# Two down projections of each feed-forward as seven half-size block products per pair of panels

## The reference

```python
# first block
h = h + (jax.nn.silu(f @ w_gate[i]) * (f @ w_up[i])) @ w_down[i]
# second block
u = causal_dwconv(h2 @ w_ff_up[l], conv_ff_w[l], conv_ff_b[l])   # 3 taps over positions
gate, val = jnp.split(u, 2, axis=-1)
x = x + (jax.nn.silu(gate) * val) @ w_ff_down[l]
```

## Time and profile before

| | us |
|---|---|
| median of 3 runs (1553.41 to 1555.92) | 1555.33 |
| span of the profiled execution | 1553.9 |
| TensorE busy in it | 1539.9 (99%) |
| GpSimd busy | 905.7 (58%) |
| Vector busy | 747.5 (48%) |
| Scalar busy | 395.1 (25%) |

### The profile page before, as it was taken

The page is one execution under the profiler, slowest core; times in us unless marked ns, Lnnn a source line. Parts: engine busy times, 40 slices in busy tenths (PEclk is TensorE's granted clock), DMA queues, the critical chain, the costliest instruction groups (busy, mean ns, idle before and its releaser), DMA issues.

```text
span 1553.9 us, 22779 instructions
## 1 busy us (share of the span) xinstructions
PE 1539.9 (99%) x7847; PEld 1291.7 (83%) x7847; DVE 747.5 (48%) x1157; ACT 395.1 (25%) x757; POOL 905.7 (58%) x536
## 2 busy tenths in 40 slices
PE   8999999999999999999999999999999999999998
PEld 7779999988888888888888888777877888888887
DVE  4157840232335354742343245868567751552456
ACT  4221210233442012210010013456564320220122
POOL 5645556544445667766666666653454666666653
PEclk9999999999999999999999999999999999999999
DMA  6223333322223432333333333322222323333322
GB/s 213 82 72 91 85 93 91 86 68 59 64 68 104 147 95 82 108 94 95 100 100 98 95 88 102 93 70 64 60 67 82 94 81 108 96 98 103 95 81 95
DMA packets 266712, 142.67 MB, mean 92 GB/s; under 512 B 6445, under 2 KB 263749, under 8 KB 266389
## 3 DMA queue, kind: packets, MB, share of 16 engines
q1 hardware_dynamic: 265285, 139.16, 30.5%
q10 hardware_dynamic: 1360, 2.56, 0.4%
HBM read 137.38 MB, written 4.19 MB: 91 GB/s over the span
## 4 chain that ended last, share of the span: by engine, by line
PE 95%; DVE 3%; ACT 1%; issue 1%; DMA 0%; ACTq 0%; DVEq 0%
PE PS L645 74%; PE PS L643 12%; PE PS L872 1%; PE PS L849 1%; PE PS L957 1%; PE PS L797 1%; DVE BL L2051 1%; PE PS L875 0%; PE PS L923 0%; PE PS L848 0%; PE PS L862 0%; DVE L L1881 0%; PE PS L1003 0%; DVE L L1864 0%; ACT SBX L1422 0%
## 5 line engine op out<-in xcount | busy, mean ns | idle before, releaser
L586 POOL TENSOR_TENSOR WL<-RAW,WH 128x1024 fp32r<-128x1024 f32 (+1 forms) x259 | 622.7, 2404 | 21.6
L584 POOL TENSOR_SCALAR WH<-RAW 128x1024 fp32r<-128x1024 f32 (+1 forms) x259 | 280.4, 1083 | 607.6 <-DMA RAW<-in_w_in_dram 257.5
L645 PE MATMUL PS<-BH,WH 128*128 128x512 f32 x928 | 366.6, 395 | 1.2 <-DVE BL L2051 1.1
L645 PE MATMUL PS<-BL,WH 128*128 128x512 f32 x928 | 361.4, 389 | 0.0
L645 PE MATMUL PS<-BH,WL 128*128 128x512 f32 x928 | 361.1, 389 | 0.0
L645 PEld LDWEIGHTS PS<-BH,WH 128*128 128x128 f32 x928 | 174.2, 188 | 42.4 <-issue 4.4
L645 PE MATMUL PS<-AH,WH 128*128 128x512 f32 x528 | 205.9, 390 | 0.0
L645 PE MATMUL PS<-AL,WH 128*128 128x512 f32 x528 | 205.4, 389 | 0.0
L645 PE MATMUL PS<-AH,WL 128*128 128x512 f32 x528 | 205.4, 389 | 0.0
L645 PEld LDWEIGHTS PS<-BH,WL 128*128 128x128 f32 x928 | 174.3, 188 | 37.2 <-issue 1.7
L645 PEld LDWEIGHTS PS<-BL,WH 128*128 128x128 f32 x928 | 174.2, 188 | 36.6
(11 more groups left out here) (334 smaller groups left out, 1817.4 us busy)
## 6 DMA issues: line engine op xcount, KB each, us to landing
RAW<-in_w_in_dram SPq DMA_DIRECT2D x89, 512.0 KB, 3.4
RAW<-in_w_ff_up_dram SPq DMA_DIRECT2D x44, 512.0 KB, 3.6
RAW<-in_w_gate_dram SPq DMA_DIRECT2D x22, 512.0 KB, 3.6
RAW<-in_w_up_dram SPq DMA_DIRECT2D x22, 512.0 KB, 3.6
RAW<-in_w_down_dram SPq DMA_DIRECT2D x16, 512.0 KB, 3.6
RAW<-in_w_ff_down_dram SPq DMA_DIRECT2D x16, 512.0 KB, 3.6
RAW<-in_w_out_dram SPq DMA_DIRECT2D x10, 512.0 KB, 3.7
RAW<-in_w_conv_out_dram SPq DMA_DIRECT2D x8, 512.0 KB, 3.7
```

Of the source, the lines that this page charges most:

```text
L584: nc.gpsimd.tensor_scalar(WH[:, slot, 0:kc], RAW[:, slot, 0:kc], 1.0, 1.0, ALU.mult, ALU.mult).then_inc(w_hi, 1)
L586: nc.gpsimd.tensor_tensor(WL[:, slot, 0:kc], RAW[:, slot, 0:kc], WH[:, slot, 0:kc].bitcast(F32), ALU.subtract).then_inc(w_ready, 1)
L645: last = mm(bank_of(name, i)[0:rows], w[:, w_at, k, 0:rows], a[:, k, :], start=st, stop=sp_)
```

## The change

The stages `dn0`, `dn1`, `ed0` and `ed1` (those over 8 chunks) are worked in four "duos" of two panels. A duo is a 2 x 2 block product: even and odd chunks of the inner dimension, its two panels, and the first and second 256 tokens. Where eight products of blocks would do the sum, seven of sums and differences do it (Strassen, in Winograd's form). Each product is four slices x 3 matmuls of 256 columns.

- Activations: for each pair of chunks seven pieces of 256 columns. `MADE1`/`MADE2` holds the even chunk and the difference of its halves; `A7` the odd chunk (two pieces) and three sums of pieces. Their high parts (`A7H`) come from Scalar, their low parts (`A7L`) from Vector.
- Weights: of a duo's two panels s0 and s1 Vector makes four sums (`add_second` three, `add_third` one) of 512 elements, one of them over half of s1's panel in `RAW`. Scalar makes all high parts (`high_first`, `high_sums`, `high_second`, `high_third`), Vector the low parts of two sums and of s1 (`low_sums`, `low_second`, 1024 elements each), GpSimd those of s0 and of the third sum (`low_first` 1024, `low_third` 512).
- Outputs: products 6 and 7 go on in the bank of product 1 (1, then 1+6, then 1+6+7). Vector adds all seven states to `H` (`evict`), two of them twice over (512 elements), the others over 256. TensorE waits for the eviction of 1 before it begins 6, and of 6 before 7.
- In the first duo of a stage products 2, 6, 3 and 4 leave their last slice for later (`EARLY_PARTS`).
- The clearing of `XA` moves from before `wo` to after `dn1`, and the semaphores of the norms are merged into shared ones; no instruction is added by either.

```diff
+DUO_STAGES = ["dn0", "dn1", "ed0", "ed1"]
+DUOS = 4
...
+DUO_ORDERS = [(1, 5, 6, 2, 3, 4, 7)] + [(1, 5, 2, 6, 4, 7, 3)] * (DUOS - 1)
+DUO_COUNTED = [[q for q in order if q not in (2, 7)] for order in DUO_ORDERS]
+PIECES = {1: 1, 5: 0, 2: 2, 3: 3, 6: 4, 7: 5, 4: 6}
+ARRIVAL = {1: 1, 5: 1, 2: 2, 3: 2, 6: 3, 7: 3, 4: 3}
+EARLY_PARTS, MADE = 3, 12
+HALF_T = T // 2
...
+            def low_first(name, n):
+                m, s = duo(name, n), duo_slots(name, n)[0]
+                pool.wait_ge(first_hi, m + 1)
+                nc.gpsimd.tensor_tensor(WAL[:, n % 2], RAW[:, s], WH[:, s].bitcast(F32), ALU.subtract).then_inc(first_lo, 1)
+            def low_third(name, n):
+                pool.wait_ge(third_hi, duo(name, n) + 1)
+                nc.gpsimd.tensor_tensor(WSL[:, n % 2, 2], WS[:, n % 2, 2], WSH[:, 2].bitcast(F32), ALU.subtract).then_inc(third_lo, 1)
+            def duo_lows(name):
+                low_first(name, 0)
+                low_third(name, 0)
+                low_first(name, 1)
+                low_third(name, 1)
+                low_first(name, 2)
+                low_first(name, 3)
+                low_third(name, 2)
+                low_third(name, 3)
+                pool.sem_inc(w_hi, COUNT[name])
+                pool.sem_inc(w_ready, COUNT[name])
...
+            def product(name, n, q, ks=range(4)):
+                m, b, (s0, s1) = duo(name, n), n % 2, duo_slots(name, n)
+                bank = duo_bank(name, n, q)
...
+                if ks[0] == 0:
+                    if q in (1, 2):
+                        pe.wait_ge(first_lo, m + 1)
+                    elif q in (5, 6):
+                        pe.wait_ge(sums_lo, m + 1)
+                    elif q == 3:
+                        pe.wait_ge(third_lo, m + 1)
+                    else:
+                        pe.wait_ge(second_lo, m + 1)
+                    if q == 6:
+                        pe.wait_ge(duo_out, 7 * m + DUO_ORDERS[n].index(1) + 1)
+                    elif q == 7:
+                        pe.wait_ge(duo_out, 7 * m + DUO_ORDERS[n].index(6) + 1)
+                    elif q == 3 and n:
+                        pe.wait_ge(duo_out, 7 * m + DUO_ORDERS[n].index(2) + 1)
+                    elif q == 1 and n == 1:
+                        pe.wait_ge(duo_out, 7 * (m - 1) + DUO_ORDERS[0].index(3) + 1)
+                    elif n == 0 and q != 3:
+                        pe.wait_ge(freed["dve"], LETGO[name]["dve"] - 3 + {1: 0, 5: 1, 2: 2, 4: 3}[q])
+                    elif n > 1:
+                        pe.wait_ge(duo_out, 7 * (m - 1))
+                pe.wait_ge(pieces_lo, MADE * DUO_STAGES.index(name) + 3 * ks[-1] + ARRIVAL[q])
...
+            def duo_stage(name):
+                early, rest = range(EARLY_PARTS), range(EARLY_PARTS, 4)
+                product(name, 0, 1)
+                product(name, 0, 5)
+                for q in (2, 6, 3, 4):
+                    product(name, 0, q, early)
+                for q in (6, 2, 3, 4):
+                    product(name, 0, q, rest)
+                product(name, 0, 7)
+                for n in range(1, DUOS):
+                    for q in DUO_ORDERS[n]:
+                        product(name, n, q)
+            def after_duos(name):
+                pe.wait_ge(duo_out, 7 * duo(name, DUOS - 1))
...
+            def high_even(g, i, src):
+                act.wait_ge(even_made, i + (DUOS * g + 1))
+                act.sem_inc(act_seen, 1)
+                go(one(A7H, i)[:, 0:2], src[:, 0:2], ACT.Copy).then_inc(pieces_hi, 1)
+            def high_odd(g, i, c0):
+                act.wait_ge(ff_step, i * 2 + (c0 + 2))
+                act.sem_inc(act_seen, 1)
+                go(one(A7H, i)[:, 2:4], one(A7, i)[:, 2:4], ACT.Copy).then_inc(pieces_hi, 1)
+                act.wait_ge(odd_made, i * 2 + (2 * DUOS * g + 2))
+                act.sem_inc(act_seen, 1)
+                go(one(A7H, i)[:, 4:7], one(A7, i)[:, 4:7], ACT.Copy).then_inc(pieces_hi, 1)
...
+            def duo_highs(name):
+                high_sums(name, 1)
+                high_second(name, 1)
+                high_third(name, 1)
+                high_first(name, 2)
+                high_second(name, 2)
+                high_sums(name, 2)
+                high_first(name, 3)
+                high_third(name, 2)
+                high_second(name, 3)
+                high_sums(name, 3)
+                high_third(name, 3)
...
+                if g < 2:
+                    with act.Fori(0, n // 2 - 1) as i:
+                        gate_tanh(i, 0)
+                        high_even(g, i, MADE1)
+                        gate_tanh(i, 1)
+                        high_odd(g, i, c0)
+                    i = n // 2 - 1
+                    gate_tanh(i, 0)
+                    high_even(g, i, MADE1)
+                    high_first(down, 0)
+                    high_sums(down, 0)
+                    high_second(down, 0)
+                    high_third(down, 0)
+                    gate_tanh(i, 1)
+                    high_first(down, 1)
+                    high_odd(g, i, c0)
+                    duo_highs(down)
+                    continue
...
+            def add_second(name, n):
+                m, (s0, s1) = duo(name, n), duo_slots(name, n)
+                dve.wait_ge(raw_loaded[s1], duo_loads(name, n)[1])
+                if m > 1:
+                    dve.wait_ge(duo_product, 5 * (m - 1))
+                tt(WS[:, n % 2, 0], RAW[:, s1, 0:KC:2], RAW[:, s1, 1:KC:2], ALU.add).then_inc(duo_added, 1)
+                dve.wait_ge(raw_loaded[s0], duo_loads(name, n)[0])
+                dve.wait_ge(duo_added, 4 * m + 1)
+                tt(WS[:, n % 2, 1], WS[:, n % 2, 0], RAW[:, s0, 0:KC:2], ALU.subtract).then_inc(duo_added, 1)
+                tt(RAW[:, s1, 0:KC:2], RAW[:, s0, 0:KC:2], RAW[:, s1, 0:KC:2], ALU.subtract).then_inc(duo_added, 1)
+            def add_third(name, n):
+                m, (s0, s1) = duo(name, n), duo_slots(name, n)
+                dve.wait_ge(duo_added, 4 * m + 2)
+                tt(WS[:, n % 2, 2], RAW[:, s0, 1:KC:2], WS[:, n % 2, 1], ALU.subtract).then_inc(duo_added, 1)
+            def low_sums(name, n):
+                dve.wait_ge(duo_added, 4 * duo(name, n) + 4)
+                dve.wait_ge(sums_hi, duo(name, n) + 1)
+                tt(WSL[:, n % 2, 0:2], WS[:, n % 2, 0:2], WSH[:, 0:2].bitcast(F32), ALU.subtract).then_inc(sums_lo, 1)
+            def low_second(name, n):
+                s = duo_slots(name, n)[1]
+                dve.wait_ge(second_hi, duo(name, n) + 1)
+                tt(WL[:, s], RAW[:, s], WH[:, s].bitcast(F32), ALU.subtract).then_inc(second_lo, 1)
...
+            def evict(name, n, q):
+                m, c = duo(name, n), 2 * n
+                if q == 2:
+                    after(name, 2 * n)
+                elif q == 7:
+                    after(name, 2 * n + 1)
+                else:
+                    dve.wait_ge(duo_product, duo_products(m, q))
...
+                if q in (5, 7):
+                    bank = bank.unsqueeze(1).to_broadcast([P, 2, HALF_T])
+                stt(out=h, in0=bank, scalar=0.5, in1=h, op0=ALU.mult, op1=ALU.add).then_inc(duo_out, 1)
...
+            def odd_pieces(g, i, c0, src):
+                dve.wait_ge(ff_step, i * 2 + (c0 + 2))
+                a = one(A7, i)
+                tt(a[:, 4], a[:, 3], src[:, 0], ALU.subtract)
+                tt(a[:, 5], a[:, 3], src[:, 2], ALU.subtract).then_inc(odd_made, 1)
+                dve.wait_ge(odd_made, i * 2 + (2 * DUOS * g + 1))
+                tt(a[:, 6], a[:, 2], a[:, 4], ALU.subtract).then_inc(odd_made, 1)
+            def low_odd(g, i):
+                dve.wait_ge(odd_made, i * 2 + (2 * DUOS * g + 2))
+                dve.wait_ge(pieces_hi, i * 3 + (MADE * g + 2))
+                tt(one(A7L, i)[:, 2:4], one(A7, i)[:, 2:4], one(A7H, i)[:, 2:4].bitcast(F32), ALU.subtract).then_inc(pieces_lo, 1)
+            def low_turned(g, i):
+                dve.wait_ge(pieces_hi, i * 3 + (MADE * g + 3))
+                tt(one(A7L, i)[:, 4:7], one(A7, i)[:, 4:7], one(A7H, i)[:, 4:7].bitcast(F32), ALU.subtract).then_inc(pieces_lo, 1)
...
+            def first_duo(name, g, i, c0, made):
+                evict(name, 0, 1)
+                odd_pieces(g, i, c0, made)
+                low_odd(g, i)
+                evict(name, 0, 5)
+                low_turned(g, i)
+                add_second(name, 1)
+                evict(name, 0, 6)
+                add_third(name, 1)
+                evict(name, 0, 2)
+                evict(name, 0, 3)
+                low_sums(name, 1)
+                evict(name, 0, 4)
+                evict(name, 0, 7)
+                low_second(name, 1)
+            def later_duos(name):
+                for n in range(1, DUOS):
+                    more = n + 1 < DUOS
+                    evict(name, n, 1)
+                    evict(name, n, 5)
+                    if more:
+                        add_second(name, n + 1)
+                    evict(name, n, 2)
```

(44 more changed lines are left out.)

338 lines of the change are left out of this document (249 added, 89 removed).

## The result

The changed kernel takes 1584.63 us (median of 4 runs, 1582.99 to 1585.74) against 1555.5 for the kernel before in the same rounds: a ratio of 1.019, 95% interval 1.0176 to 1.0204, **29 us slower**. The forecast was 1572.7 with a range of 1546 to 1586. The profiled execution has a span of 1581.3 us, 27.4 over that of before.

A forecast was written before the change was run, and what follows sets the result against it. TensorE was taken to bound the kernel; 15.5 us saved there, less waits behind Vector and GpSimd, gave 2.9 more in each `dn` and 5.8 in each `ed`: 17.4 us more, 1572.7 us, range 1546 to 1586.

The forecast's parts named there:

- What bounds the kernel: Whole kernel: TensorE sets the time, busy for 99% of the span and holding 95% of the chain.
- the rule on which all hung: Changed stages: Vector and GpSimd exclude each other when Vector reads two SBUF operands, up to 12.1 us a duo against 9.9.
- TensorE's pace, 0.118: Changed stages: 0.118 us per matmul of 256 columns, 39.6 us a stage against 43.5, four stages saving 15.5.
- The 109 ns by the Trainium skill: Changed stages: the skill's time for a matmul of 256 columns, a saving of 19 us; set aside for the trace.
- The entry to `dn`: `dn` stages: waits behind Vector and GpSimd of 6.8 us, a stage of 46.4 us, 2.9 more than before.
- The entry to `ed`: `ed` stages: waits of 9.7 us with the later duos, a stage of 49.3 us, 5.8 more than before.
- panel 13's chain ends at -6.4: Entry to `ed`: Vector's steps for panel 13 end 6.4 us before the stage's first matmul is due.
- 2.5 more: Entry to `ed`: 2.5 us more if the taps of the chunk before are late too, left to the range.
- The sum: Whole kernel: 2 x 2.9 + 2 x 5.8 = 17.4 us more, profiled execution from 1553.9 to 1571.3.
- Vector keeps ahead: `dn` and `ed`: GpSimd's steps always fall in Vector's gaps; -3.5 and +1.7 a stage, sum -3.6, 1551.7 us; 20%.
- The clock falls as well: Stage entries: waits lower TensorE's clock; 40 matmuls at twice 0.118 cost 4.7 us a stage, 1591 us; 5%.

The follow-up runs named there:

- e3: Changed kernel without GpSimd's two subtractions in the duo stages, the high part multiplied again instead: 1566.69 us, ratio 1.0095 to the kernel before.
- e6: Changed kernel with duos in `dn` only, plus 14 matmuls into an unused bank ahead of product 6: 1556.87 us, ratio 1.0022 to the kernel before.
- e12: Changed kernel without GpSimd's duo subtractions and without low parts in the `gv` loops, a copy for the norm's reciprocal: 1559.55 us, ratio 1.0035 to the kernel before.
- e7: Changed kernel, duos in `dn` only, Scalar's high part for duo 1 later, product 6's eviction before the next duo's first sum: 1559.87 us, ratio 1.0048.
- e8: Changed kernel, duos in `dn` only, GpSimd's low parts made by Vector, sums behind two evictions, Scalar's first high part sooner: 1557.84 us, ratio 1.0029.
- e10: As e8 (`dn` only, all low parts on Vector) with three steps placed otherwise: 1551.53 us, ratio 0.9988 to the kernel before.
- e4: Changed kernel with Scalar's high part of duo 1's first panel issued after those of the odd chunk: 1586.07 us, ratio 1.0199 to the kernel before.
- e9: Changed kernel with duos in `dn` only and Scalar's high part of duo 0's first panel one step sooner: 1557.62 us, ratio 1.0031 to the kernel before.
- e2: Changed kernel with duos in `ed0` and `ed1` only, `dn` in panels as before: 1573.23 us, ratio 1.0122 to the kernel before.
- e11: Changed kernel with a copy in place of the reciprocal of the norm ahead of `gv0`: 1578.93 us, ratio 1.0162 to the kernel before.

## Why the prediction was right in its sign and short in its size

- **What bounds the kernel, and the rule on which all hung:** right. With GpSimd's steps out, TensorE ran through `dn1` without a stop (e3).
- **TensorE's pace, 0.118:** the term was mis-sized. Its rows were 0.2267 for 512 columns and 0.1208 for 258: the slope between them is 0.417 ns a column, with 13 ns in every matmul, which gives 0.120 for 256. Measured: 336 in 40.3 us in `dn1` of e3, 0.120. A stage needs 40.3 and not 39.6, and the four save 12.8 and not 15.5. The 109 ns by the Trainium skill ("TensorE: Matmul & The Clock Gate") were further off; the saving of 19 us beside them sets them against the 216 ns of the same page, and against this trace's 43.5 us a stage it would be 27.5.
- **The entry to `dn`:** right step by step. Product 6: 2.9 forecast, 2.3 measured; product of the last chunk out at 6.2, measured 5.8; last low parts 10.0, measured 9.4; before product 7: 1.0, 1.8, 0.8 forecast for duos 0 to 2, 0.9 (e6), 1.4 and 0.35 measured. The stage was +2.1 for +2.9.
- **The entry to `ed`:** +4.2 and +5.7 for +5.8, behind the wait of product 1, so near in sum, and in part by luck. Product 6: 3.0 forecast, 2.1 and 2.6 measured. Product 5: 1.7 and 0.3. Some 1.5 us in each are the half clock, which the sum did not have. By e12 (+4.0 and +2.6 with GpSimd's steps out) more of it is Vector's own list than the port. Product 1, which was to wait 0.5, waited 10.4 and 2.6; the table has that in `gv0` and `gv1`.
- **The step that failed** is "panel 13's chain ends at -6.4": it let Vector enter the last pass of `gv` on time and priced that pass alone. Two of the three passes ahead of it had grown from 17.0 to almost 24 us in `gv0`, so that the late start behind the norm was still there at their end. Even in `gv1` Vector scaled panel 12 at 1409.36, 5.3 us after TensorE was done with it. Lateness was in the text only as "2.5 more", left to the range; it was 11.8 at `gv0` and 2.8 at `gv1`, half of the 27.4.
- **The sum:** -12.8 on TensorE, +10.6 in the two `dn` stages (45.6 less 40.3 each), +16.3 in the two `ed` stages, +14.6 at the ends of `gv0` and `gv1`, -1.3 elsewhere: 27.4, as the spans differ. Forecast: -15.5, +13.6, +19.4, 0.
- **The rivals.** "Vector keeps ahead" did not come about in `dn`, where it would have needed e3's Vector. "The clock falls as well" did, at a smaller price: 15 matmuls in each `dn` stage, 18 in `ed0` and some 15 in `ed1`, and e6 shows for `dn` that little of it is net. The Trainium skill ("TensorE: Matmul & The Clock Gate", on oscillation) has the clock fall to 1.2 GHz where TensorE's work in a loop has gaps; this trace agrees after single gaps of 2.3, 2.6 and 10.4 us, and in the five traces four of ten gaps of 2.25 to 2.6 us came without it.

## What to carry to other kernels

Halving the matmuls is paid for by the engines that make the operands. Before costing the stage that changes, cost the loop ahead of it: compare each helper's time for a pass, before and after, with TensorE's for the same pass, and ask what late start the slack of the old passes was making good, since lateness hides in the buffers and comes out at the next change of stage. Where two engines exclude each other, add their times and give the work to the one that does it faster (some 2 us between e7 and e8; e10 has a better order as well). With the work left where it was, an order that freed one waiter found another (e4, e7, e9).

## What had not been expected of the hardware

- After TensorE had stood for 2.3 us the granted clock was 0.50 from 706.2 to 709.6, although TensorE was busy again, and after 10.4 us of standing it was 0.50 up to 1289.7; 14 matmuls into an unused bank kept it at 1.00 in `dn`.
- Matmuls of 256 columns start 0.213 us apart at the granted clock 0.50 and 0.117 to 0.120 apart at 1.00, which is more than half.
- The same list of Vector steps beside the same list of GpSimd steps took 62 to 67.5 us for three passes in five kernels (after, e2, e3, e4, e11).
